# Sample attention in 64-row TensorE tiles, differential row sums as 32-column tiles, two output buffers, and closing steps above the exponentials, in an eight-core transformer layer

## What is computed

```python
x += 0.5 * gate1 * SwiGLU_1(RMSNorm(x) * (1 + scale1) + shift1)      # D 1024, D_FF 2816
h  = RMSNorm(x) * (1 + scale2) + shift2
dq, dk, dv, gq, gk, gv = split(h @ w_in)      # 4 differential heads, 8 GQA heads on 2 kv heads, dim 64
# differential head: two softmaxes of 64-dim keys, one 128-dim value
a = softmax(q0 @ k0.T / 8) - lam * softmax(q1 @ k1.T / 8)
o_diff = rmsnorm(a @ v) * 0.8
o_gqa  = softmax(gq @ gk.T / 8) @ gv          # q and k with RMSNorm
x += gate2 * concat(o_diff, o_gqa) @ w_out
x += 0.5 * gate3 * SwiGLU_2(RMSNorm(x) * (1 + scale3) + shift3)
y  = RMSNorm(x)
```

## Time and profile before

| | |
|---|---|
| median of 3 runs | 3947.0 us (3945.17 to 4084.97) |
| the profiled execution | 3947.68 us, span of its slowest core 3946.2 us, 1.5 us around it |
| spans of the 8 cores | 3928.2 to 3946.2 us |
| granted PE clock, mean | 0.961 of full speed |
| DMA | 572.79 MB, mean 145 GB/s |

### The profile page before, as it was taken

The page is one execution under the profiler, slowest core; times in us unless marked ns, Lnnn a source line. Parts: engine busy times, 40 slices in busy tenths (PEclk is TensorE's granted clock), DMA queues, the critical chain, the costliest instruction groups (busy, mean ns, idle before and its releaser), DMA issues.

```text
span 3946.2 us, 51478 instructions; the slowest of 8 cores (3928.2 to 3946.2 us)
## 1 busy us (share of the span) xinstructions
PE 3505.6 (89%) x15812; PEld 1523.4 (39%) x15812; DVE 2322.3 (59%) x3013; ACT 2048.4 (52%) x2608; POOL 99.9 (3%) x183
## 2 busy tenths in 40 slices
PE   1996899998869698998999999899989999899988
PEld 0442344443334344444334444333423433334433
DVE  5665774543554755565755676655567655655643
ACT  2213323334443434443576766677776667777631
POOL 0000000001010000000000000000000000000000
PEclk9998899999989799999999999999999999999989
DMA  8787776666536267565523423422233313332232
GB/s 215 174 208 203 210 259 186 197 210 168 166 110 187 77 179 213 176 206 198 165 88 112 136 81 115 152 92 79 90 115 133 106 63 105 133 104 86 89 124 95
DMA packets 134842, 572.79 MB, mean 145 GB/s; under 512 B 16848, under 2 KB 22480, under 8 KB 129744
## 3 DMA queue, kind: packets, MB, share of 16 engines
q1 hardware_dynamic: 118304, 491.56, 37.6%
q0 software_dynamic: 16272, 77.93, 9.2%
HBM read 540.40 MB, written 90.51 MB: 160 GB/s over the span
## 4 chain that ended last, share of the span: by engine, by line
PE 65%; ACT 15%; DVE 9%; issue 6%; DMA 4%; ACTq 0%; DVEq 0%; SPq 0%; POOL 0%; POOLq 0%
PE PSA L464 65%; ACT PT L467 10%; ACT L467 2%; DVE RG L470 1%; DVE MT L473 1%; DVE XB L473 1%; ACT HB L467 1%; DVE FIN L477 1%; DVE FIN L484 1%; DMA DR<-w_dn 1%; DVE PT L473 1%; DMA PT<-w_ada 1%; DVE NS L470 1%; ACT FIN L467 1%; DMA s_vd<-RG 1%
## 5 line engine op out<-in xcount | busy, mean ns | idle before, releaser
L464 PE MATMUL PSA<-HB,WR 128*128 128x512 bf16 x6800 | 1577.4, 388 | 143.1 <-ACT HB L467 58.4
L467 ACT ACTIVATE PT<-PSA 128x1024 bf16<-128x1024 f32 x1184 | 1151.5, 1021 | 344.3 <-PE PSA L464 324.0
L464 PEld LDWEIGHTS PSA<-HB,WR 128*128 128x128 bf16 x6800 | 669.9, 99 | 1025.9 <-issue 290.4
L464 PE MATMUL PSA<-QTS,RG 128*128 128x512 bf16 (+1 forms) x2432 | 659.4, 375 | 74.5 <-ACT PT L467 70.8
L464 PE MATMUL PSA<-PT,RG 128*128 128x512 bf16 (+1 forms) x2368 | 648.4, 381 | 28.8 <-DVE FIN L477 22.8
L464 PE MATMUL PSA<-HID,DR 128*128 128x512 bf16 x2640 | 590.8, 380 | 17.3 <-DMA DR<-w_dn 13.9
L467 ACT ACTIVATE TH<-PSA 128x512 f32<-128x512 f32 x352 | 209.6, 596 | 576.5 <-PE PSA L464 566.9
L473 DVE SCALAR_TENSOR_TENSOR TH<-TH,PSA 128x512 f32<-128x512 f32 x352 | 241.3, 686 | 343.4 <-ACT TH L467 339.6
L464 PEld LDWEIGHTS PSA<-HID,DR 128*128 128x128 bf16 x2640 | 258.0, 98 | 333.5 <-issue 26.1
L464 PEld LDWEIGHTS PSA<-QTS,RG 128*128 128x128 bf16 (+1 forms) x2432 | 195.1, 97 | 467.8 <-issue 333.6
L467 ACT ACTIVATE SQ<-XB 128x512 f32<-128x512 f32 x224 | 139.5, 627 | 431.0 <-DVE XB L473 392.6
(11 more groups left out here) (89 smaller groups left out, 1655.9 us busy)
## 6 DMA issues: line engine op xcount, KB each, us to landing
WR<-s_gu SPq DMA_DIRECT2D x308, 512.0 KB, 4.1
DR<-s_dn SPq DMA_DIRECT2D x112, 704.0 KB, 4.6
RG<-s_kt SPq DMA_DIRECT2D x64, 576.0 KB, 4.1
WR<-s_in SPq DMA_DIRECT2D x65, 512.0 KB, 5.6
RG<-s_vg SPq DMA_DIRECT2D x32, 864.0 KB, 6.4
PT<-w_ada SPq DMA_DIRECT2D x48, 512.0 KB, 8.2
RG<-s_vd SPq DMA_DIRECT2D x32, 576.0 KB, 4.8
XB<-xs SPq DMA_DIRECT2D x8, 2048.0 KB, 9.9
```

Of the source, the lines that this page charges most:

```text
L464: return ("pe", (lambda e: e.matmul(out, lhsT, rhs, start=start, stop=stop)), reads, [PK(bank)], c, None, mode)
L467: return ("act", (lambda e: e.activation(out, in_, func, **kw)), reads, writes, 0.18 + n * 0.00082, None)
```

## The change

1. Scores: per 2 key tiles and 256 queries (`NST` = 18 steps for each half `qh` of the queries) four matmuls of 64 key rows and 256 columns: head m reads partitions 64m to 64m+63 and writes bank 2sp+m. `QTS` holds queries without zeros, one load in place of two.
2. Values: 64-row tiles as well; the lower 64 keys add up in bank 4, the upper in bank 5, so `fin_evac` copies one and adds the other. A unit closes twice, once for each half of the queries.
3. Row sums of differential units: matmuls of `PT` against 32 columns of ones, 4 for each pair of steps, into the four 32-partition groups of one bank, and from there by ACT to `ACC`; one fp32 matmul sums over the partitions. `att_acc` and the second accumulator go.
4. Two output buffers `OES` in `FIN`; the lock "FIN" is taken after the copy. Closing streams have priority 2 in place of 5.
5. Keys and values load in thirds with 3 buffers in place of halves with 2.
6. Fillers need credits: `credit` gives one for each second step, at most two are kept. One filler bank at a time (`FIL`).
7. Start: the first pair's squares are summed on PE (`stats_pe`), 16 fp32 matmuls; casts of weight blocks 2 and up wait for modulation vector 0, as do the write-backs of the first six; the second x tile loads later; the silu is issued first, lambda's small operations after vector 0.
8. The bias add of the second feed-forward's norm moves from ACT to DVE.

```diff
-    KVK_AP = [RG[:, b * 5760:b * 5760 + 2304] for b in range(2)]
+    KVK_AP = [RG[:, b * 3840:b * 3840 + 1536] for b in range(3)]
...
-            gate = [("MOD", 1)] if kind == "gu0" else [("HID", 10)] if kind == "dn0" else []
+            gate = [("MOD", 1) if idx < 2 else ("MOD", 0)] if kind == "gu0" else [("HID", 10)] if kind == "dn0" else []
...
-                if (m, c) in ((1, 3), (0, 1)):
+                if (m, c) in ((1, 3), (0, 7)):
...
+    def stats_pe(xb):
+
+        b = yield Get("bank")
+        for c in range(8):
+            s = yield Get("SQ")
+            yield [act(SQ[:, s, :], XB[:, xb, c, :], AF.Square, [("X", xb, c)], [("SQ", s)])]
+            yield [mm(PSB[b], ONESF[:, :], SQ[:, s, :], [("SQ", s), "ONESF"], b, start=(c == 0), stop=(c == 7), cost=0.9)]
+            put("SQ", s)
+        put(("stp", xb), b)
...
+                if i == 2:
+                    yield [ts(HB[:, h, c, :], MT[:, c % 2, :], MOD[:, g, 24 * i + c:24 * i + c + 1], None, ALU.add, None,
+                              [("MT", c % 2), ("MOD", 3 * i)], [("H", h, c)], n=512)]
+                    continue
...
+    def spend():
+        yield Get("cr")
+        if short[0]:
+            put("cr")
...
+    def credit(kind, st):
+
+        n = 2 if st == NST - 1 else st % 2
+        while n and len(S.pools["cr"]) < 2:
+            n -= 1
+            put("cr")
...
-                    yield [mm(PSB[2 * sp + m], KVK_AP[ks][:, kk * 128:(kk + 1) * 128], QTS[:, 2 * sl + m, :],
-                              [("KVK", ks), ("QT", 2 * sl + m)], 2 * sp + m) for m in range(2)]
...
+                        yield [mm(PSB[2 * sp + m][:, 256 * kt:256 * kt + 256], KVK_AP[ks[th]][64 * m:64 * m + 64, (2 * r + kt) * 128:(2 * r + kt + 1) * 128],
+                                  QTS[64 * m:64 * m + 64, c, 256 * qh:256 * qh + 256], [("KVK", ks[th]), ("QT", c)], 2 * sp + m, cost=0.054, mode=1)
+                               for kt in range(2) for m in range(2)]
...
-                        yield [tt(ACCS[e], ACCS[e], PT[:, p, :], ALU.add, [("ACC", e), ("PT", p)], [("ACC", e)], n=960)]
...
+                        yield [mm(PSB[b][32 * (2 * e + kt):32 * (2 * e + kt) + 32, :].rearrange("p (m n) -> p m n", m=2), ONESB[:, 0:32],
+                                  PT[:, ps[e], :].rearrange("p (m k n) -> p k m n", m=2, k=2)[:, kt], [("PT", ps[e]), "ONESB"], b,
+                                  start=(i == 0), stop=(i == NST // 2 - 1), cost=0.103, mode=2) for e in range(2) for kt in range(2)]
...
+                    yield [act(ACC[:, 0:512], PSB[b], AF.Identity, [PK(b)], [("ACC", 0)], scale=1.0 / 32)]
...
+        yield [cp(OES[x], PSB[4], [PK(4)], [("OE", x)] + first, n=512)]
+        yield [tt(OES[x], OES[x], PSB[5], ALU.add, [PK(5), ("OE", x)], [("OE", x)])]
+        put("PV")
...
+                            if kind == "d":
+                                for t in range(2):
+                                    g.append(mm(PSB[4 + t].rearrange("p (m n) -> p m n", m=2), V[64 * t:64 * t + 64, kk * 128:kk * 128 + 128],
+                                                Pk[64 * t:64 * t + 64, kt], reads, 4 + t, start=a, stop=z, cost=0.108, mode=1))
...
-                S.spawn(fin_d(q, u, ot) if kind == "d" else fin_g(q, u, ot), A_PRIO)
+                    S.spawn(fin_d(q, u, qh, ot) if kind == "d" else fin_g(q, u, qh, ot), 2)
```

238 lines of the change are left out of this document (151 added, 87 removed).

## The result

The changed kernel takes 3,895.5 us (median of 4 runs) against 3,947.0: a ratio of 0.9869, with a 95% interval of 0.9846 to 0.9891. On the chip of a later comparison it was 0.9849 (0.9827 to 0.9872). The gain is real and smaller than 2%, for which I had given a chance of 0.39, and 0.55 for more; I forecast 3,848, so 47 us of it are missing. In some executions the cores of a die run longer at a lower clock; every ratio here compares executions without that. The profiled execution took 3,898.1 us with a span of 3,896.6, on core 2.

The account below looks back on a forecast made before the run. TensorE (PE) was taken as the bound where fillers run in attention. 3947.7 - 180 (attention) + 112 (tail) - 12 (fewer fillers ahead of attention) - 20 (start) = 3,847.7, forecast 3848 us; range 3735 to 3970.

Parts of the forecast that it names:

- What bounds: Sample attention: PE is the bound where feed-forward work fills in; its matmuls make 1,641 of the 1,827 us.
- the 85 I named: Sign in attention: the prediction is wrong if ACT is over 85% busy there.
- ACT takes over: Rival in attention: ACT cannot catch up after filler bursts, remainder 270 us instead of 210, total 3,908; chance 0.25.
- Scores, values, row sums, change of form: PE in attention: scores 249 us (minus 248), values 498 (nothing gained), row sums 62, about 1,060 form changes 106.
- column tiles do not overlap: Rival on attention's row sums: four tiles run in turn, 248 us instead of 62, total 4,034; chance 0.07.
- the pairs don't keep up: Rival on attention's scores and values: 0.125 us a pair under continuous weight loads, total 3,966, no change; chance 0.08.
- Fillers: Feed-forward matmuls: 2,194 in attention, 474 us, and 1,142 in the tail, 506 more than before, 109 us.
- Closings and waits: Attention's remainder of small waits and gaps, 186 us before: could become 100 to 270, taken as 210, plus 24.
- closings were the hidden cost: Rival in attention: two buffers and priority remove nearly all stalls, remainder 100 us, total 3,738; chance 0.18.
- Row sums on DVE: Attention: 544 DVE adds of 1.22 us and 32 casts go; DVE loses 664 us of adds.
- Start: Before the first real matmul: later casts and squares on PE save 20 us, bounds 0 and 27.
- Ahead of attention: Stretch before sample attention: 56 fewer fillers stand there, minus 12 us.

Follow-up runs that it names:

- experiment 6: Changed kernel with the sums stream's PSUM bank freed until attention, each group of four column tiles issued twice: 0.9856 of the kernel before.
- experiments 2 and 9: 2: changed kernel, fillers without credits, 0.9893 of before. 9: changed kernel with the bank freed, a credit every step instead of every second, 0.9767.
- Experiment 5: Changed kernel with the bank freed, differential row sums left as DVE adds, no column tiles: 1.0074 of the kernel before.
- experiment 1: Start alone, both ways: changed kernel with the old start, 0.9894 of before; kernel before with the new start, 0.9957.
- experiment 4: Changed kernel, sums stream taking its PSUM bank only when attention opens: 3,863.4 us, 0.9771; kernel before with one bank held until then: 3,966.2 us.

## Why the prediction was right and where it was not

The case I forecast is the one that came: TensorE led in the mean, and the range held. The 47 us that are missing lie in no term of attention. By the prediction's own steps:

*What bounds.* Right in the mean: ACT is busy for 1,322 of 1,673 us of attention, 79%, under the 85 I named, and still waits for PE. But the mean hides two kinds of half unit. On core 3 of the changed kernel, 15 of the 32 differential half units hold few fillers (9 in the mean); they last 18.9 us each with ACT busy for 94% and PE for 97% of it. In the other 49 ACT is busy for 76 to 78%. So *ACT takes over* came in part: in some 280 us of attention ACT is as good as full, and PE's wait for exps doubled to 97 us. The Trainium skill, page "TensorEngine Tiling (Array Packing)", section "PSUM Bottleneck", says that tiling does not speed up what empties PSUM. The traces agree for the half units with few fillers (ACT busy for 17.86 of 18.65 us in experiment 6) and not for those with many (21.50 of 28.69).

*Scores, values, row sums, change of form.* Right. 0.108 a pair under continuous loads, 0.209 to 0.22 a group of four column tiles, 0.10 to 0.11 a change, and 1,067 changes in the built order where I counted about 1,060. The rivals *column tiles do not overlap* and *the pairs don't keep up* are out. The Trainium skill's 2.38 for three column tiles (page "TensorE: Matmul & The Clock Gate", section "Measured speedup vs the span model"), by which I had estimated 0.27 us a group, does not fit four tiles here: 0.209 is the full overlap.

*Fillers.* Mis-sized. I took 2,194 in attention and 1,142 in the tail; the built order has 2,320 and 1,016 (the order printed with the change already adds up to 1,016 behind the last scores), and the trace 1620 + 704 = 2,324 and 662 + 352 = 1,014. I misread the order by 126. 130 x 0.216 = 28 us go back from the tail to attention: 1,647 + 28 = 1,675, measured 1,673.4; 302 - 28 = 274, measured 273.6. The sum of both never depended on it. That the tail costs about what attention saves is shown by experiments 2 and 9.

*Closings and waits.* The remainder of 210 us was right in size: 249 + 498 + 62 + 48 + 106 + 2,324 x 0.216 = 1,465, and 1,673 less that is 208. But it was taken near the middle of 100 and 270, and what the edits do in it I had not seen, so that it met is in good part luck. Without their rank the two stretches cost 275 us more, without the second buffer 81 more. I had listed 22.8 us of shown waits as the evidence against them; in the new layout, with 64 closings instead of 32, the closings are the first danger, and rank and buffer are what keeps the remainder as it was. That they protect the gain and don't add one fits this; the rival *closings were the hidden cost*, which had the remainder at 100, did not come either.

*Row sums on DVE.* I priced them at 62 us of PE work and gave what leaves DVE no number of its own. Experiment 5 gives some 100 us for it, net of the tiles, in the layout with cheap scores. Had the adds stayed, the remainder would have grown. DVE's busy time fell from 2,322 to 1,772 us, 550 where I had said about 600.

*Start.* Right in its way and near in size: 10 to 18 us by the ratios of experiment 1, of 20.

*Ahead of attention: the step that failed.* "56 fewer stand ahead of attention: minus 12" took stage one to be otherwise untouched. It was not: the new stream of sums holds one of six PSUM banks from the first microsecond. Mean over the cores, attention began at 1,921 before and at 1,929 after, where minus 32 would have been 1,889; on the slowest cores it is 1,930.2 and 1,949.6, since the cores of a die now lie 16 to 36 us apart there and not 14 to 16. With the bank freed they still lie 22 and 30 apart, and what spreads them stays open. Freeing the bank brings the mean from 1,929 to 1,907, 22 us (experiment 4), and 3 to 6 more behind it. The 18 from there to 1,889 can be read off too. The new start alone brings the kernel before from 1,921 to 1,908, 13 us where I had 20. The kernel with the bank freed has the same order up to its 7,465th matmul, then 40 fillers fewer, and begins at 1,907: 1.6 us earlier, where 56 fillers fewer were to save 12. So fewer fillers ahead of attention saved almost nothing of their price; why, no run shows.

The miss could have been seen: the built orders of before and of the changed kernel with the old start part at the 1,319th matmul of stage one, a group of keys and values (near 434 us), where the diff touches nothing. I read the order only at the places that the change names.

## What to carry to other kernels

When a planner or a pool hands out buffers, a new stream's first request counts from the moment it is planned, not from the moment it is needed. After adding one, compare the order of the stretches that the change should not touch; any difference there is a cost to be explained, and no wait in a profile names a buffer that somebody else holds. And when the bound engine's work is cut in half by tiling, first ask which small chains (closings, accumulators) stay at their old price: here they decided over up to 275 us, the halved scores, by the prediction's sum, over 248.

## What the hardware showed that I had not expected

Four column tiles of 32 columns run together without loss: doubling 1,152 of them added 60.2 us, 52 ns a tile, when one alone has a record of 388 ns. A change of tile form costs 0.10 to 0.11 us in every direction seen, from 64 rows to full, from column tiles to 64 rows and back.

Table loads on ACT more than doubled in attention, from 28 (35.9 us) to 62:

```profile
L467 ACT ACT_TABLE_LOAD x62 | 79.5, 1283 | 11.6 <-PE PSA L464 10.3
```

They are 44 us more, of ACT's 1,322. What they cost no run shows; they would count in half units where ACT is the bound.

In the kernel with late closings the granted clock of TensorE is 0.94 over attention, where it is 0.99 with the closings first. In pieces of 50 us of core 3, the five lowest (0.80 to 0.86) are pieces in which PE was busy for only 30 to 41 us. Waits on PE's path were paid twice, once as idle time and once in the clock: 59 us more of busy time for 183 fillers fewer.
